# A later place for fewer blocks: reordering the end of an expert layer, and constant products at three norms

## The reference

```python
for i in range(2):                                   # first model
    x = x + merged @ w_o[i]                          # two attention branches, gated
    x = x + hierarchical_moe(rmsnorm(x, g_ffn[i]), ...)   # 32 experts, 2 per token
    ple_gate = sigmoid(rmsnorm(x, g_ple[i]) @ w_ple_gate[i])
    x = x + (p[i] @ w_ple[i]) * ple_gate             # p: the per-layer embedding
x = rmsnorm(x, g_final)
h = rms_norm(x, g_mix_2)                             # second model, one layer
x = x + merged @ w_out                               # three branches
u = rms_norm(x, g_ffn_2) @ w_gu
x = x + (silu(gate) * up) @ w_down
return rms_norm(x, g_final_2)
```

## Time and profile before

| | us |
|---|---|
| median of 3 runs | 2428.04 (2426.86 to 2429.57) |
| the profiled execution | 2430.51 |
| its span, first to last instruction | 2428.7 |
| PE busy | 2286.0 (94%) |
| DVE busy | 1001.9 (41%) |
| ACT busy | 586.9 (24%) |
| POOL busy | 411.5 (17%) |
| mean granted clock of PE | 0.982 |

### The profile page before, as it was taken

How to read it: one execution, slowest core, us unless ns; L and a number is a source line. 1 busy time by engine, 2 the same in 40 slices (tenths; PEclk the granted TensorE clock), 3 DMA queues, 4 the chain that set the end, 5 groups by cost and what they waited for, 6 DMA issues and landing times. The chain is left out here.

```text
span 2428.7 us, 29699 instructions
## 1 busy us (share of the span) xinstructions
PE 2286.0 (94%) x11860; PEld 1698.3 (70%) x11860; DVE 1001.9 (41%) x1763; ACT 586.9 (24%) x1210; POOL 411.5 (17%) x407
## 2 busy tenths in 40 slices
PE   7989999997889989999998888999989999999998
PEld 6667788654457767788754446877768887888887
DVE  5544533511145454643521126445653435332234
ACT  3533401311133342410311115223540002000012
POOL 2011111122211101111122121111101121111211
PEclk9999999999999999999999999999999999999999
DMA  5114536799961202233899982322213332333322
GB/s 162 51 47 107 130 111 251 320 421 423 418 234 56 70 20 79 66 96 137 330 420 422 422 328 89 91 84 81 83 42 96 94 115 78 96 97 100 98 96 71
DMA packets 291930, 396.57 MB, mean 163 GB/s; under 512 B 32590, under 2 KB 232014, under 8 KB 274378
## 3 DMA queue, kind: packets, MB, share of 16 engines
q1 hardware_dynamic: 274880, 366.27, 42.1%
q0 software_dynamic: 11328, 16.81, 1.9%
q10 hardware_dynamic: 5578, 11.51, 1.8%
HBM read 388.98 MB, written 30.15 MB: 173 GB/s over the span
## 5 line engine op out<-in xcount | busy, mean ns | idle before, releaser
L146 PE MATMUL banks<-h_split,w_high 128*128 128x512 f32 x2624 | 825.6, 396 | 2.8 <-PEq L3325 1.7
L146 PEld LDWEIGHTS banks<-h_split,w_high 128*128 128x128 f32 x2624 | 481.0, 188 | 104.3 <-issue 8.2
L198 DVE TENSOR_TENSOR w_low<-w_raw,w_high 128x1024 fp32r<-128x1024 f32 (+1 forms) x264 | 317.1, 1201 | 503.5 <-POOL w_high L187 503.5
L187 POOL CAST w_high<-w_raw 128x1024 fp32r<-128x1024 f32 (+1 forms) x264 | 277.7, 1053 | 1455.5 <-PE banks L146 1325.5
L146 PE MATMUL banks<-h_split,w_low 128*128 128x512 f32 x1312 | 512.1, 390 | 0.0
L146 PEld LDWEIGHTS banks<-h_split,w_low 128*128 128x128 f32 x1312 | 246.3, 188 | 52.6
L146 PE MATMUL banks<-w_high,op_split 128*128 128x512 f32 x736 | 228.5, 390 | 1.6 <-DVE mg_part L1358 1.1
L2091 PE MATMUL banks<-expert_ring,ex_xsT 128*64 128x256 f32 x1408 | 172.7, 401 | 32.9 <-DMA expert_ring<-in_w_exp_up 32.9
L2091 PEld LDWEIGHTS banks<-expert_ring,ex_xsT 128*64 128x64 f32 x1408 | 102.4, 144 | 90.9 <-DMA expert_ring<-in_w_exp_up 36.1
L146 PEld LDWEIGHTS banks<-w_high,op_split 128*128 128x128 f32 x736 | 138.2, 188 | 32.1 <-DVE mg_part L1358 2.4
L146 PE MATMUL banks<-w_low,op_split 128*128 128x512 f32 x368 | 143.2, 389 | 0.0
(11 more groups left out here) (448 smaller groups left out, 2740.1 us busy)
## 6 DMA issues: line engine op xcount, KB each, us to landing
w_raw<-in_w_in SPq DMA_DIRECT2D x142, 512.0 KB, 3.9
expert_ring<-in_w_exp_gate SPq DMA_DIRECT2D x42, 1024.0 KB, 20.6
expert_ring<-in_w_exp_up SPq DMA_DIRECT2D x42, 1024.0 KB, 23.8
expert_ring<-in_w_exp_down SPq DMA_DIRECT2D x42, 1024.0 KB, 23.6
region<-in_w_exp_gate SPq DMA_DIRECT2D x22, 1024.0 KB, 19.8
region<-in_w_exp_up SPq DMA_DIRECT2D x22, 1024.0 KB, 23.7
region<-in_w_exp_down SPq DMA_DIRECT2D x22, 1024.0 KB, 23.6
w_raw<-in_w_gu SPq DMA_DIRECT2D x44, 512.0 KB, 4.0
```

Source lines behind the costliest of these rows:

```text
L146: last = nc.tensor.matmul(out, left, right, start=(start and n == 0), stop=(stop and n == 2), skip_group_check=True)
L187: self.nc.gpsimd.tensor_copy(self.high[:, i % self.SPLIT, 0:n], self.raw[:, i % self.RAW, 0:n]).then_inc(self.high_ready, 1)
L198: self.nc.vector.tensor_tensor(self.low[:, i % self.SPLIT, 0:n], self.raw[:, i % self.RAW, 0:n], self.high[:, i % self.SPLIT, 0:n].bitcast ...
```

## The change

Four edits, with the rest following from them.

1. `ORDER` puts the overflow block behind block 27, no longer behind block 29. POOL issues the refills one block earlier, and the lists of which tokens form a pair are adapted (DVE instructions of the same number).
2. SP issues the embedding's weights first, and the gate's behind them, after one more block's down products (expert 28 is now the block at position 29).
3. Four embedding products stand ahead of the border and four behind it, before three and five.
4. Constants' products at the norms: 17 in `LateNorm`, 25 in `FinalNorm`, 8 in `second_half`.

```diff
-    late = True
+    late, unread = True, 17
@@ class FinalNorm(LateNorm)
+    unread = 25
@@ merge_and_route, sync
-            sp.wait_ge(e.down_done, EXPERTS - 3)
-            gate_stream.loads(sp, 0, gate_stream.RAW)
             for q in (e.pairs - 2, e.pairs - 1):
                 c = (q + 1) % GATHERS
                 sp.wait_ge(e.turned, 2 * q + 2)
                 sp.dma_start(*embedding.load_pair(c)).then_inc((p_landed0, p_landed1)[c], 16)
+            sp.wait_ge(e.down_done, EXPERTS - 2)
+            gate_stream.loads(sp, 0, gate_stream.RAW)
             e.stored(sp)
@@ constants
-ORDER = (*range(EXPERTS - 2), EXPERTS, EXPERTS - 2, EXPERTS - 1)
+ORDER = (*range(EXPERTS - 4), EXPERTS, *range(EXPERTS - 4, EXPERTS))
-EARLY_PRODUCTS = 3
+EARLY_PRODUCTS = 4
@@ Experts.pooled
-            if refill_ready and n == RESIDENT:
+            if refill_ready and n == RESIDENT - 1:
                 pool.wait_ge(refill_ready, 1)
                 self.refill_gate_up(pool, last_weight_row[0])
-            if refill_ready and n == RESIDENT + 1:
+            if refill_ready and n == RESIDENT:
                 self.refill_down(pool, last_weight_row[1])
@@ embed_per_layer, tensor (its end)
+        pe.wait_ge(sig_done, 1)
+        unread(k, 0, late.unread)
@@ second_half, tensor (ahead of norm.open_tiles)
+            pe.wait_ge(op.added, 1)
+            unread(k, 0, 8)
```

More of the change, by code:

```diff
@@ L1865, in _ @@
             halves = tuple(enumerate((slice(0, LANES), slice(LANES, P))))
-            last_pairs = ((15, 16, (EXPERTS, EXPERTS - 2)), (16, 17, (EXPERTS - 1, EXPERTS + 1)))
+            resident_pair = EXPERTS, EXPERTS - 4
+            last_pairs = slice(EXPERTS - 3, EXPERTS, 2), slice(EXPERTS - 2, EXPERTS + 2, 3)
             for half, lanes in halves:
-                V.tensor_scalar(r.token[lanes, 0:15], k.ps[lanes, 7, half:EXPERTS - 2:2], 2.0 * S, None, ALU.add)\
+                V.tensor_scalar(r.token[lanes, 0:14], k.ps[lanes, 7, half:EXPERTS - 4:2], 2.0 * S, None, ALU.add)\
                     .then_inc(token_ready, 1)
             for half, lanes in halves:
-                for start_at, stop_at, blocks in last_pairs:
-                    V.tensor_scalar(r.token[lanes, start_at:stop_at], k.ps[lanes, 7, blocks[half]:blocks[half] + 1], 2.0 * S, None,
-                                    ALU.add)
+                V.tensor_scalar(r.token[lanes, 14:15], k.ps[lanes, 7, resident_pair[half]:resident_pair[half] + 1], 2.0 * S, None,
+                                ALU.add)
+                V.tensor_scalar(r.token[lanes, 15:17], k.ps[lanes, 7, last_pairs[half]], 2.0 * S, None, ALU.add)
                 V.tensor_scalar(r.token[lanes, 17:], k.ps[lanes, 7, EXPERTS + half:BLOCKS:2], 2.0 * S, None, ALU.add)
```

## The result

| | before | changed |
|---|---|---|
| median of 5 runs, us | 2429.47 (2426.86 to 2432.02) | 2415.60 (2414.76 to 2420.62) |
| ratio | | 0.9948, interval 0.9936 to 0.9959 |
| the profiled execution, us | 2430.51 | 2415.53 |
| its span | 2428.7 | 2413.7 |
| PE busy | 2286.0 | 2291.1 |

13.9 us were won by the medians, 12.6 by the ratio (which is not the quotient of the two medians) and 15.0 by the two profiled spans; the forecast was 15.3 off 2428.04, the median of the first three runs: 2413, with a range of 2408.5 to 2419.5. The total hides that two of its terms were too large, one of them by far, and that in the profiled pair something else made up for them. So the stages come one by one, each by its own length and not by where it stands.

What follows compares the result with a forecast made beforehand. PE, busy for 94% of the span, was taken to bound the kernel through its waits and half-clock stretches. Terms 2.5 + 3.5 + 2.5 + 6.85 = 15.3 us off the median 2428.04 gave 2413, range 2408.5 to 2419.5.

Steps and rivals of the forecast that it cites:

- The overflow block, layer one: End of expert layer one: expert 31 starts at 678.2, limited by its up weights, not at 680.70; gain 2.5 us.
- the low-clock case of the prediction: Layer one, expert 31: the wait for its up weights brings half clock, and the gain is only 0.8 us.
- Layer two: End of expert layer two: refill replaces the weights' wait, expert 31 starts at 1429.3, not 1432.81; gain 3.5 us.
- The refill's price: Refills ahead of the overflow block land in 8.2 to 10.7 us; down refills cost nothing or about 1 us, once.
- The rival in which it turns the kernel slower: Expert layers: refills taking 22 us delay the queued experts, 21.3 us lost, 9.35 won, time 2440; chance 0.04.
- the rival in which nothing shows: Whole kernel: the clock falls and the border eats the layers' gains, time 2427; chance 0.03.
- The order on SP: Embedding's weights ahead of the gate's: worth 0.2 us by itself, avoids a wait of 2.7 us; cost 0 to 1.5.
- Four products: Border of the expert layers: the fourth early product hides, three tiles' transposes run during DVE's additions; gain 1.3 us a layer.
- Constants' products: Three norms: filling PE's idle stretches wins back half clock, 2.65 + 2.9 + 1.3, together 6.85 us; bounds 0 and 8.3.
- What they can give back is half clock: Step at the three norms: half clock behind each idle stretch becomes full clock once constants' products fill it, 6.85 us.
- the clock falls all the same: Norms: PE's clock drops in the thin stretch behind the constants' products, 6.85 becomes about 0.5, time 2419; chance 0.2.
- a clock of 0.5 behind the constants' products: Sign at the norms that the forecast is wrong: PEclk of 0.5 after the constants' products, where 1.00 was forecast.

Runs made afterwards that it cites:

- b2: The changed kernel without the four refill DMAs and the waits for them; 2417.09 us, ratio 0.9939 to the kernel before.
- a1: The changed kernel without its three sets of constants' products at the norms; 2424.29 us, ratio 0.9978 to the kernel before.
- a4: The changed kernel with the gate's weights issued ahead of the embedding's, both behind the later block; 2425.71 us, ratio 0.9984 to the kernel before.
- b1: The kernel before with only the overflow block's new place, its refills and token lists, and both weight loads behind the later block; 2425.81 us, ratio 0.9991.
- c0: The changed kernel run once more, nothing altered; 2417.03 us, ratio 0.9947 to the kernel before.
- d1: The kernel before with only the 17, 25 and 8 constants' products added at the norms; 2424.47 us, ratio 0.9985.
- b3: The changed kernel with constants' products also between and behind the norms' transposed tiles, 12 for 8 ahead of the feed-forward's norm; 2415.77 us, ratio 0.9938.
- b6: b3 with five more constants' products ahead of the border and five behind each of the third and fourth tiles' transposes; 2416.76 us, ratio 0.9945.
- b4: The changed kernel with seven more constants' products ahead of the second model's last values projection; 2420.72 us, ratio 0.9971 to the kernel before.
- a2: The changed kernel with the overflow block back behind block 29, refills and token lists as before; 2424.68 us, ratio 0.9985 to the kernel before.

## Why the prediction was right, and which steps weren't

**The overflow block, layer one: right, with some luck.** 2.3 us for 2.5. Position 32 was limited by the transfer, with 0.25 us of waiting, at 677.73 for a forecast of 678.2. The slack of 2.5 us that the sum gave PE was not there, since position 28 started 1.7 us later than forecast; the refill had no part in that, it landed at 650.4 (642.16 and 8.2). In ten profiles with the new place it started between 677.3 and 680.2, though nine of them (all but b2) issue the same PE instructions from the routing to there. So a gain as small as in the low-clock case of the prediction (0.8) happens too, by later weights rather than by the clock: in a1 and a4 position 26 is already 3.1 us late.

**Layer two: right in size.** 3.8 for 3.5. The refill did take the place of the wait for weights (1.27 us); b2 shows it. The forecast had both limits, the refill with the blocks behind it and expert 31's up weights, at the same moment, 1429.3. So it is: without the refill 1.3 us were saved at the one place and 1.9 us waited at the other, and the two limits lie within a microsecond of each other. Two sizes in the sum were off and nearly cancelled: the second refill was issued 7.5 us behind position 26's start (6.9 forecast), and block 32 started 7.9 us after that (8.8 forecast).

**The refill's price: right.** 7.0 to 8.2 us from issue to landing in the changed kernel's profile (up to 9.3 in others), for 8.2 to 10.7 before. The rival in which it turns the kernel slower fell, and so did the rival in which nothing shows.

**The order on SP: right, and the most useful step.** I put 0.2 us on it by itself and 2.7 us on its absence. Its absence cost 2.43 and 2.84 us of waiting in a4 and 2.92 and 3.14 in b1, and b1 shows that the place without it wins 2.2 us in all.

**Four products: mechanism right, size too large.** 1.05 and 0.95 us for 1.3. The twelve other transposes hide wholly, and the last tile's start on DVE, 10.57 us behind the border, as forecast (10.5). What the 1.3 left out is that these four take 0.71 us alone, where as the tail of sixteen they add 0.45 (1.95 less 1.50). From b1 comes a limit: with full clock behind the border three early products do as well.

**Constants' products: the term that failed.** 6.85 us were forecast, 2.65 + 2.9 + 1.3; the changed kernel's profile gave 2.5 + 1.25 + 0.05 = 3.8. The failing step is "What they can give back is half clock", where I took it as given back each time once the idle stretch was filled. The sizes were near, 6.2 for 6.85: where the clock holds, the three stretches take 15.32, 13.55 and 8.41 us (c0), which against before is 2.5 + 2.8 + 0.9. In all eight profiles of kernels with these sets (and no fill behind them) the first norm takes 15.3 us; without them 16.3, 17.8 and 18.4. Between the models five of the eight lost clock behind the set (14.8 to 16.1 us, against 13.55), before the feed-forward two of eight (9.3 against 8.4; without a set 9.2 to 9.4 in three of three). The mean of the eight is 15.33, 14.60 and 8.63, that of the three without 17.48, 15.75 and 9.29: 2.15 + 1.15 + 0.66, which is 4.0 us. My sum counted full clock at all three as certain; it held in eight of eight at one, in three of eight and six of eight at the others. The rival "the clock falls all the same" had the mechanism for a part of the executions at two of three places; d1's 3.6 us by the ratio is near this 4.0. One of the forecast's own signs of being wrong, a clock of 0.5 behind the constants' products, was there, though the total came out in the range. In b3 and b6, which fill the thin stretches as well, the clock is 1.00 at all three norms, two profiles of two.

The rule on transposes from "TensorE: Matmul & The Clock Gate" of the Trainium skill, Part 4 (PE-mode transpose), would have had the clock fall at the first norm too. There the trace disagrees: the 16 transposes of 759.29 to 763.06, 2.48 us of work, stand between the constants' products and the first projection at a clock of 1.00 in the windows above. Before the feed-forward the changed kernel's trace is mixed: the clock fell while such transposes ran, from some 2041.4 on, as the rule would have it, but with nothing else on PE it was back at 1.00 from 2044.8, when the last had ended. In six of the eight profiles it did not fall there.

**What made up for it.** 2.2 us in the window attention, which no edit touches and where I forecast nothing, and 0.9 scattered. The stretch takes 6.4 us in nine profiles, 7.5 in two (b3, b4), 8.6 in two (before, b2). What sets it no run here tells, nor how often the kernel before has 8.6, of which there is one profile. In the profiled pair the right total owes 2 us to it, and that is luck; without it the time would still lie in the range, near 2418.

**What stays open.** Whether the constants' sets win 3.6 us or 7.3 (alone, or in the changed kernel); what sets the length of the window attention's last turns; why position 26 of layer one comes 3 us late in some executions; what decides, within one kernel, at which thin stretch the clock falls.

## What to carry to other kernels

When work is moved so that a wait goes, ask at once which transfer is late next, and move its issue forward in the same edit: the place alone won 2 us, and without the order of the weights behind it 8.7 of the changed kernel's 12.6 us were lost, with the two borders 5.9 us later in the profile. A filled gap held the clock in every profile only at one norm of three, and at all three once the thin stretch behind it was filled too (two profiles), so count such a gain by how often it comes and not at its best. Read a stage's length and not its position, and look at a second execution before a stage of the profile is called a gain.

## What the runs showed that I had not expected

- *The same kernel loses its clock at different places.* Three stages of the changed kernel differ by 0.9 to 1.6 us between two executions, in both directions, and the spans by 0.7 us. What decides it is open.
- *A faster stretch ahead of a wait can cost.* Where the four products behind the border ran at full clock, 7.13 us, PE idled for 1.93 us and the gate's products lost 1.3 to 2.8 us: five layers of five (a2, a4, b2). Where they took 8.8 us it was 2 of 10. In b6, which fills the wait, they took 7.13 us in layer two and the gate's products lost nothing.
- *Refills that fetch nothing are not free.* With all of their indices out of bounds they land 7.0 to 10.7 us after the issue, and each takes POOL 1.0 us to issue. Leaving them out (b2) changed the time by nothing that can be told.
